# One VectorE instruction of each feed-forward step moves up: the corner operand's remainder, from behind the next step's operands to between the pairs of operand sums

## The reference

```python
def _swiglu(x, w_gate, w_up, w_down):
    return (jax.nn.silu(x @ w_gate) * (x @ w_up)) @ w_down
...
    for l in range(DEPTH):
        ...
        x = x + (gate_a * branch_a + gate_b * branch_b) @ w_o[l]
        x = x + _swiglu(_rmsnorm(x, norm2_g[l]), w_ffn_gate[l], w_ffn_up[l], w_ffn_down[l])
    return x
```

## Time and profile before

| | us |
|---|---|
| median of 3 runs | 1540.76 (1539.07 to 1541.68) |
| profiled execution | 1541.02 |
| its span | 1539.2 |

### The profile page before, as it was taken

How to read it: one execution, slowest core, us unless ns; L and a number is a source line. 1 busy time by engine, 2 the same in 40 slices (tenths; PEclk the granted TensorE clock), 3 DMA queues, 4 the chain that set the end, 5 groups by cost and what they waited for, 6 DMA issues and landing times.

```text
span 1539.2 us, 23039 instructions
## 1 busy us (share of the span) xinstructions
PE 1492.0 (97%) x8954; PEld 1221.1 (79%) x8954; DVE 1085.8 (71%) x1470; ACT 677.4 (44%) x1167; POOL 425.9 (28%) x232
## 2 busy tenths in 40 slices
PE   8999999999999999999999999899999999999998
PEld 3555888778788878888888888787888988988987
DVE  5999888677448986658323971786888875886684
ACT  4564168742452232232333223787346552553351
POOL 0000053454443455444443324345540000000000
PEclk9999999999999999999999999999999999999999
DMA  6568720232242244453528632004331332233223
GB/s 245 163 206 294 288 70 1 69 107 72 96 139 82 91 170 141 151 157 96 167 96 294 209 134 89 28 1 114 120 94 44 106 128 69 83 109 125 69 83 123
DMA packets 73499, 189.51 MB, mean 123 GB/s; under 512 B 23600, under 2 KB 32176, under 8 KB 69296
## 3 DMA queue, kind: packets, MB, share of 16 engines
q1 hardware_dynamic: 41952, 145.18, 28.3%
q10 hardware_dynamic: 31440, 42.87, 8.7%
HBM read 155.52 MB, written 32.51 MB: 122 GB/s over the span
## 4 chain that ended last, share of the span: by engine, by line
PE 62%; DVE 19%; DVEq 5%; DMA 4%; ACT 4%; issue 4%; POOLq 1%; POOL 1%; SPq 0%; ACTq 0%
PE ps L2164 18%; PE ps L2166 18%; PE ps L2165 18%; DMA stage<-in_stream 2%; DMA stage_more<-in_stream 2%; PE ps L2313 2%; DVE wl L2010 2%; DVE work L1393 1%; ACT prob L1147 1%; PE ps L2219 1%; PE ps L2290 1%; DVEq L1573 1%; DVE wl L2015 1%; DVEq L1520 1%; PE ps L2258 1%
## 5 line engine op out<-in xcount | busy, mean ns | idle before, releaser
L636 POOL TENSOR_TENSOR wl<-stage,wh 128x1024 fp32r<-128x1024 f32 x138 | 356.8, 2592 | 644.9 <-ACT wh L729 454.9
L729 ACT ACTIVATE wh<-stage 128x1024 fp32r<-128x1024 f32 (+2 forms) x178 | 181.0, 1023 | 221.6 <-PE ps L2166 102.4
L2164 PE MATMUL ps<-XH,wh 128*128 128x256 f32 x616 | 176.7, 287 | 16.2 <-DVE wl L2010 11.5
L2166 PE MATMUL ps<-XH,wl 128*128 128x256 f32 x616 | 173.6, 282 | 0.0
L2165 PE MATMUL ps<-XLr,wh 128*128 128x256 f32 x528 | 148.7, 282 | 0.0
L2164 PE MATMUL ps<-xg2h,wh 128*128 128x512 f32 x352 | 140.2, 398 | 0.0
L2165 PE MATMUL ps<-xg2l,wh 128*128 128x512 f32 x352 | 139.2, 395 | 0.0
L2166 PE MATMUL ps<-xg2h,wl 128*128 128x512 f32 x352 | 139.2, 395 | 0.0
L2164 PEld LDWEIGHTS ps<-XH,wh 128*128 128x128 f32 x616 | 116.7, 189 | 22.2 <-DVE wl L2010 15.1
L2166 PEld LDWEIGHTS ps<-XH,wl 128*128 128x128 f32 x616 | 116.8, 190 | 0.0
L2219 PE MATMUL ps<-X,slabs 128*128 128x512 f32 x224 | 101.7, 608 | 5.9 <-DMA X<-in_xT 5.0
(11 more groups left out here) (346 smaller groups left out, 3652.3 us busy)
## 6 DMA issues: line engine op xcount, KB each, us to landing
stage<-in_stream SPq DMA_DIRECT2D x178, 512.0 KB, 3.5
stage_more<-in_stream SPq DMA_DIRECT2D x34, 512.0 KB, 4.0
CPTR<-ctd_scr ACTq DMA_DIRECT2D x6, 1664.0 KB, 7.8
slabs<-in_stream SPq DMA_DIRECT2D x17, 512.0 KB, 5.1
InT<-in_scr ACTq DMA_DIRECT2D x6, 1024.0 KB, 6.6
ctd_scr<-CPp SPq DMA_DIRECT2D x4, 1152.0 KB, 7.8
ctd_scr<-CPp ACTq DMA_DIRECT2D x4, 1152.0 KB, 6.6
in_scr<-BPI SPq DMA_DIRECT2D x4, 1024.0 KB, 5.1
```

The lines of the kernel that those rows point to most:

```text
L636: pool.tensor_tensor(wl[:, s, :], stage[:, (n - RAW) % STAGES, :], wh[:, s, :].bitcast(F32), ALU.subtract).then_inc(wl_ready, 1)
L729: return act.activation(o, i, ACT.Copy, **kw)
L2164: pe.matmul(o, wt[0], x[0], start=start, stop=False, skip_group_check=onto)
L2166: return pe.matmul(o, wt[1], x[0], start=False, stop=stop, skip_group_check=onto)
```

## The change

`corner_low(q)` is called right behind `sums_first(q+1)` (and, in step 0, `first_sum`), ahead of `sums_last(q+1)`, and no more at the list's end.

```diff
--- before.py
+++ after.py
@@ -2115,6 +2115,7 @@
                         sums_first(q + 1)
                     if q == 0:
                         first_sum(q)
+                    corner_low(q)
                     if q < last:
                         sums_last(q + 1)
                     if q == 1:
@@ -2127,7 +2128,6 @@
                     else:
                         down_low(h, 0)
                         down_low(h, 1)
-                    corner_low(q)
                     if q == 0:
                         dve.wait_ge(rms_ready, 2 * l + 2)
                         dve.reciprocal(rscol[:], rscol[:]).then_inc(rs_ready, 1)
```

## The result

| | before | after |
|---|---|---|
| median | 1540.85 (4 runs, 1539.07 to 1541.68) | 1590.92 (4 runs, 1588.80 to 1593.54) |
| profiled execution, its span | 1541.02, 1539.2 | 1590.36, 1588.6 |
| TensorE busy | 1492.0 | 1513.5 |
| mean granted clock | 0.997 | 0.982 |

The kernel is slower by 50 us: the ratio is 1.0327 [1.0309, 1.0346]. The forecast was 1577 with a range of 1565 to 1584, so the time lies 7 us above the range. The sign and the chain were right; the clock's part was not: TensorE's clock fell to half more often than was said. (A *fall* is a stretch in which the granted clock is 0.5.) It came out as in the rival in which nearly every step falls (1592).

A forecast was written before the change was run, and what follows sets the result against it. Two chains meeting on VectorE were taken to bound the kernel: the corner operand's load, and the work behind the sums. From the median 1540.8, +27 us for the chain and +9 for clock falls gave 1577 us, range 1565 to 1584.

The forecast's parts named there:

- nearly every step falls: Rival on TensorE's clock: a step waiting at the same place may fall each time, 1592 us; chance 0.12.
- The load's wait goes: VectorE's line 1995, a step's first operand sum: the earlier load removes its wait, up to 2.3 us a step.
- Line 2015 waits for ScalarE and is the chain's new member: The moved corner remainder on VectorE waits some 2.5 to 3.5 us in each step with a successor.
- The step, 12.46 even and 12.55 odd: Feed-forward step length in us at full clock, through TensorE, ScalarE and VectorE; mean 12.5 against 11.1 before.
- The wait before P1, 2.25, 16 times: TensorE waits about 2.25 us before the first product of 16 steps, about 36 us in all for line 2010.
- The sum of the chain, 27: Longer steps, part entries and last steps of the feed-forward's three parts add 27 us, without the clock.
- step 2 to step 7: First part's term: from 55.20 before to 62.48, three even and two odd steps, +7.28 us.
- The wait of P4 for line 2090 goes: TensorE's 0.52 us wait in odd steps disappears, as line 2090 ends 0.6 earlier.
- The clock, six falls, +9: Six of TensorE's 16 new waits bring a fall to half clock, 1.5 us each, +9 us.
- 0.6 of the way: Where a 2.25 us wait was placed towards the shortest that brought a fall; basis for taking six falls.
- 1568: Time in us of the rival in which TensorE's clock holds, without falls in the steps; chance 0.28.
- by that rule this rival would be the forecast: Prediction's reading of the skill's loop that lost the clock every pass; it would favour 1592, chance 0.12.

The follow-up runs named there:

- high_early: Kernel after, with ScalarE's high(3, q), the corner's high part, moved ahead of first_corner(q), the copy that waits for P2: 1528.54 us, ratio 0.9901.
- high_early_before: Kernel before, VectorE's list unchanged, with ScalarE's high(3, q) moved ahead of first_corner(q): 1540.75 us, ratio 0.9994.
- fill9: Kernel after, with nine small matmuls into an unused bank ahead of P1 in the 16 steps that wait: 1569.46 us, ratio 1.0171.
- fill4: Kernel after, with four small matmuls ahead of P1 in the 16 steps that wait: 1585.92 us, ratio 1.0265.
- chain5: Kernel after, with five small matmuls ahead of P2, lengthening the 16 steps that lead into a long wait: 1593.28 us, ratio 1.0331.
- fill5: Kernel after, with five small matmuls ahead of P1 in the 16 steps that wait: 1574.02 us, ratio 1.0197.
- behind_scaled: Kernel before, with the corner's remainder moved behind scaled(q - 1) and ahead of low(0, q + 1): 1524.18 us, ratio 0.9877.
- after_again: Kernel after, unedited, run once more for the falls in other executions: 1590.94 us, ratio 1.0321.

## Why the prediction was right in its chain and wrong in its sum

- **The load's wait goes.** Right: no wait of line 1995 for a load is left in the kernel after.
- **Line 2015 waits for ScalarE and is the chain's new member.** Right in kind: 2.46 in the step without a fall (2.5 to 3.5 were said), 4.95 with one. high_early and high_early_before show that this wait decides: with the high part early the same list of VectorE gains 1%.
- **The step, 12.46 even and 12.55 odd.** Right: 12.44 even and 12.59 odd. The piece from the remainder's start to line 2001 is 0.61, and from there to P1 3.96.
- **The wait before P1, 2.25, 16 times.** Right: 2.23 to 2.24 in 15 places, 2.59 in one, 36 us together. In all, TensorE waits 41.3 - 11.5 = 30 us more for line 2010.
- **The sum of the chain, 27.** Right: 28.1 in the profile of fill9, 26.4 by its ratio. Of the terms, step 2 to step 7 gained 1265.01 - 1196.67 = 68.34 with four falls, which less 4 x 1.45 is 62.5 (62.48 was said).
- **The wait of P4 for line 2090 goes.** Nearly: 0.2 is left in two places, in the last steps of the first two parts.
- **The clock, six falls, +9.** Wrong, and this is most of the error: 13 falls, +18.6, so 9.6 of the 14 us between 1577 and 1591. The single fall was sized right (1.5, measured 1.43; a step with one is 13.96, 14 was said). The count failed, in the step that read a wait of 2.25 as lying "0.6 of the way" from 1.72, which brought no fall, to 2.56, which did, and then took six, though 0.6 of 16 is 9.6. Two things stood against that reading. The limit in this loop is much lower than half-way: nine falls behind 15 waits of 1.75, none behind 15 of 1.65, so 2.23 was well beyond it. And the waits are not independent draws: the place of one fall on its step goes with whether the next wait has one (18 of 18 and 0 of 5 above). Nor was 2.56 a sure limit: that same wait ahead of step 0's P5 brought a fall in the profile of before and none in that of after (granted clock 1.00 from 1173.37 to 1176.78). For a loop with the step and the wait of this one, nearly all of the 16 or none was the better guess, which is 1592 or 1568; counts in between came near the limit (fill4) and with another step length (chain5).
- **The rival "nearly every step falls", 1592**, was given 0.12 on the argument that a wait of 2.25 can be over before its fall is due. The runs show why this doesn't save it: the fall comes though the wait is over, 0.72 us after P1's start at 1223.12. Then the slow stretch lies wholly in the products, on the chain. The Trainium skill ("TensorE: Matmul & The Clock Gate", section "HAM oscillation — how this bites in real kernels") tells of a loop that lost the clock in every pass. This trace agrees as to the pattern, with 13 and 14 of 16 waits. But the page's loop waited some 3 to 5 us a pass, longer than any of the 16 here. So "by that rule this rival would be the forecast" took more from the page than it says: that waits of 2.23 us are enough is shown by this trace alone.
- What remains: the chain's 28.1 against 27, and 2.7 us ahead of the feed-forward in the profiled execution, from a fall that is not of the change. Without those 2.7 the time would still be above the range.

Open: why the wait into step 13 is 2.59 (and 2.00 for 1.64 in fill5); the number of falls in executions without a profile, which only their mean clock hints at (0.978 to 0.983); and why a fall that comes ahead of P1 spares the next wait.

## What to carry to other kernels

Before an instruction is moved up in an engine's list, look at when the last semaphore that it waits for comes, and at what is queued behind it: here 3 us of wait for ScalarE were put ahead of the 4 us on which TensorE starts, while one or two places further down had the whole gain of the early load (behind_scaled, 1.2% faster) and nothing of the wait. A wait of TensorE that repeats in every pass of a loop is to be priced with the clock's fall in nearly all passes and in none, and the two times kept apart as cases. Where such a wait can't be removed, a few small matmuls on operands that lie ready can give back the fall: nine of them in each of 16 waits took 21 us off.

## What the runs showed of the hardware

- Repeated waits of TensorE of 1.75 to 1.77 us, with 11 to 12 us of dense work between them, brought the clock down in nine of 15 cases (fill4); waits of 1.63 to 1.65 in none of 15 (fill5). Between the two lies 0.1 us. A single wait of 1.72 elsewhere brought no fall, and one of 2.56 brought one in before and none in after.
- The fall may come after the wait is over: 0.72 us into the products at 1223.12, and 1.4 us into them at 1378.30 in fill5 (the matmul at 1379.70 is the first that takes longer).
- Falls in a loop come in a rhythm: one that started behind P1's start was followed by another at the next wait in 18 of 18 cases, one that took in all of P1 in none of five (after, after_again).
- Work whose results nobody reads can hold the clock: fill9 is faster than after by 1590.92 - 1569.46 = 21 us with 144 matmuls more.
- Which instruction follows matters for what a short VectorE instruction costs: a 128x512 remainder took 0.61 to the start of the next sum, and 0.78 ahead of the scaling.
